# The shared expert's down products, moved from the combination into the first two passes of the expert loop

## The reference

```python
x = layer_norm(DEEPNORM_ALPHA * x + ffn, ln2_g[i], ln2_b[i])
# ffn, in moe_ffn, for each of 64 experts, with the tokens that chose it (6 experts a token):
hb = jax.nn.silu(xb @ w_gate[eb]) * (xb @ w_up[eb])
yb = hb @ w_down[eb]                      # weighed by the token's gate, and added up
shared = (jax.nn.silu(x2 @ w_sh_gate) * (x2 @ w_sh_up)) @ w_sh_down
return acc[:T] + shared
```

## Time and profile before

| | us |
|---|---|
| median of 3 runs | 2179.4 (2177.65 to 2179.82) |
| span of the profiled execution | 2182.5 |
| PE busy | 1923.4 (88%) |
| DVE busy | 802.0 (37%) |
| expert loop, first layer, first gate product to last down product | 431.0 to 975.0 |
| expert loop, second layer | 1571.8 to 2127.3 |

### The profile page before, as it was taken

The page is one execution under the profiler, slowest core; times in us unless marked ns, Lnnn a source line. Parts: engine busy times, 40 slices in busy tenths (PEclk is TensorE's granted clock), DMA queues, the critical chain, the costliest instruction groups (busy, mean ns, idle before and its releaser), DMA issues. The chain is left out here.

```text
span 2182.5 us, 32986 instructions
## 1 busy us (share of the span) xinstructions
PE 1923.4 (88%) x11132; PEld 1122.2 (51%) x11133; DVE 802.0 (37%) x2138; ACT 374.2 (17%) x840; POOL 292.3 (13%) x375
## 2 busy tenths in 40 slices
PE   9999999799888888788999779999799888877787
PEld 4575545356545554344444368865356454544443
DVE  3101643533222222226367644524533222222226
ACT  2001641011111110010344412211011011100011
POOL 6000000011111111110017231100011111111110
PEclk9999899899999999999999589998899999999999
DMA  6210110899999999965222110012769999999966
GB/s 232 77 59 9 69 63 39 307 351 421 418 421 390 421 392 421 421 269 226 68 71 65 25 26 1 21 58 108 303 257 419 421 421 391 421 421 422 420 286 274
DMA packets 143416, 540.50 MB, mean 248 GB/s; under 512 B 30814, under 2 KB 68246, under 8 KB 93550
## 3 DMA queue, kind: packets, MB, share of 16 engines
q1 hardware_dynamic: 122030, 489.14, 55.9%
q0 software_dynamic: 21312, 50.37, 6.1%
HBM read 521.06 MB, written 45.61 MB: 260 GB/s over the span
## 5 line engine op out<-in xcount | busy, mean ns | idle before, releaser
L632 PE MATMUL bank<-W,XT 128*64 128x256 f32 x4608 | 533.0, 387 | 102.2 <-DMA W<-in_w_exp_up_dram 46.9
L632 PEld LDWEIGHTS bank<-W,XT 128*64 128x64 f32 x4608 | 355.6, 139 | 301.1 <-DMA W<-in_w_exp_gate_dram 75.1
L667 PE MATMUL bank<-W,ht 128*64 128x512 f32 x1152 | 277.8, 626 | 43.5 <-DMA W<-in_w_exp_down_dram 38.6
L667 PEld LDWEIGHTS bank<-W,ht 128*64 128x64 f32 x1152 | 86.9, 143 | 177.0 <-issue 134.7
L1858 PE MATMUL bank<-XT,rin_w 128*128 128x512 f32 x352 | 156.5, 599 | 0.0
L1151 PE MATMUL bank<-XT,foxw 128*128 128x512 f32 x320 | 137.8, 592 | 0.0
L643 DVE TENSOR_TENSOR gu<-sig,bank 128x256 f32<-128x256 f32 x72 | 30.3, 421 | 287.3 <-ACT sig L639 287.2
L645 DVE TENSOR_TENSOR h<-gu,bank 128x256 f32<-128x256 f32 x72 | 30.3, 421 | 243.2 <-PE bank L632 243.1
L1858 PEld LDWEIGHTS bank<-XT,rin_w 128*128 128x128 f32 x352 | 66.4, 192 | 83.7 <-issue 83.3
L618 ACT ACTIVATE XT<-bank 128x512 f32<-128x512 f32 x74 | 44.2, 597 | 378.3 <-PE bank L610 378.3
L1151 PEld LDWEIGHTS bank<-XT,foxw 128*128 128x128 f32 x320 | 60.6, 190 | 76.4 <-issue 76.4
(11 more groups left out here) (409 smaller groups left out, 2497.6 us busy)
## 6 DMA issues: line engine op xcount, KB each, us to landing
W<-in_w_exp_gate_dram SPq DMA_DIRECT2D x128, 1024.0 KB, 18.7
W<-in_w_exp_up_dram SPq DMA_DIRECT2D x128, 1024.0 KB, 20.8
W<-in_w_exp_down_dram SPq DMA_DIRECT2D x128, 1024.0 KB, 18.9
W<-y_rows SPq DMA_DIRECT2D x8, 2048.0 KB, 15.4
foxw<-in_fox_w_in_dram SPq DMA_DIRECT2D x13, 1024.0 KB, 5.4
rin_w<-in_rwkv_w_in_dram SPq DMA_DIRECT2D x22, 512.0 KB, 4.1
W<-y_rows SPq DMA_DIRECT2D x8, 1024.0 KB, 22.2
w_out<-in_w_out_dram SPq DMA_DIRECT2D x1, 4096.0 KB, 13.0
```

The lines of the kernel that those rows point to most:

```text
L632: last = pe.matmul((gate, up)[m][64 * a:64 * a + 64, :], xt[s][:, k, 64 * a:64 * a + 64], K.W[:, w, a, m, k * FE:(k + 1) * FE], start=(k = ...
L667: last = pe.matmul(B[5 + half][64 * a:64 * a + 64, :], ht[:, j, 64 * a:64 * a + 64], K.W[:, w, a, 2, at:at + 512], start=(j == 0), stop=(j ...
```

## The change

- The 16 shared down products of a layer go from the combination into passes 0 and 1 of the expert loop, in 8 pieces of two matmuls, 4 pieces a pass. A piece is half a tile of tokens' output (128 x 512) in bank 4. In each pass the pieces stand behind `gate_up`, behind `turn_x`, behind `turn_h` and behind `down`. Both layers do this.
- Behind each piece DVE does `X = alpha * X + bank 4` on that half tile (one scalar_tensor_tensor of 128 x 512). PE starts a piece only when DVE has added the one before (`shared_added`).
- The four scalings of X by alpha go from the combination, and each routed sum starts its bank anew.
- The slots' numbers move from bank 4 to the free half of bank 7, which the up products use; PE therefore waits for `index_made` ahead of the up products.
- In pass 0, `slot_rows` and `index_rows` for pass 2 move behind the third piece.

```diff
@@ expert_loop
-        slots = B[4][:, 0:4]
+        slots = B[7][:, FE:FE + 4]
@@ gate_up
             for m, done in ((0, gate_done), (1, gate_up_done)):
+                if m:
+                    pe.wait_ge(index_made, n + 3 if not early(n) or n else 2)
@@ new
+        def shared_product(pe, piece):
+            t, half = divmod(piece, 2)
+            if piece == 0:
+                pe.wait_ge(shared.loaded, 16)
+            else:
+                pe.wait_ge(shared_added, piece)
+            for j in range(2):
+                last = pe.matmul(B[4][:], shared.hidden[:, j, t * P:(t + 1) * P], shared.w[:, j, half * 512:(half + 1) * 512],
+                                 start=(j == 0), stop=(j == 1))
+            last.then_inc(shared_made, 1)
+
+        def add_shared(dve, piece):
+            t, half = divmod(piece, 2)
+            dve.wait_ge(shared_made, piece + 1)
+            x = K.X[:, t, half * 512:(half + 1) * 512]
+            dve.scalar_tensor_tensor(x, x, ALPHA, B[4][:], ALU.mult, ALU.add).then_inc(shared_added, 1)
+
+        def early(n):
+            return isinstance(n, int)
@@ PE, from_slot
                         gate_up(pe, u, n, pair, w)
-                        if isinstance(n, int) and n == 0:
+                        if early(n):
+                            shared_product(pe, 4 * n)
+                        turn_x(pe, 1 - u, n + 1)
+                        if early(n):
+                            shared_product(pe, 4 * n + 1)
+                        turn_h(pe, n)
+                        if early(n):
+                            shared_product(pe, 4 * n + 2)
+                        if early(n) and n == 0:
                             slot_rows(pe, 0, 2)
-                        turn_x(pe, 1 - u, n + 1)
-                        turn_h(pe, n)
                         slot_rows(pe, 1 - u, n + 3)
                         down(pe, n, pair, w)
+                        if early(n):
+                            shared_product(pe, 4 * n + 3)
@@ DVE, one_pass (index_rows for pass 2 goes from ahead of the loop to here)
                     hidden(dve, n, step)
+                    if early(n):
+                        add_shared(dve, 4 * n)
                     keep_xt(dve, 1 - u, n + 1, 1)
+                    if early(n):
+                        add_shared(dve, 4 * n + 1)
                     keep_ht(dve, n)
-
+                    if early(n):
+                        add_shared(dve, 4 * n + 2)
+
+                    if early(n) and n == 0:
+                        index_rows(dve, 0, ahead[1][:, 2:3], 2, step)
...
                     keep_y(dve, u, n, 1)
+                    if early(n):
+                        add_shared(dve, 4 * n + 3)
@@ Combination.products
-        pe.wait_ge(self.scaled, 1)
-        pe.wait_ge(self.diagonals, 1)
-        pe.wait_ge(shared.loaded, 16)
...
-        for t in range(NT - 1):
-            shared_product(t)
-        pe.wait_ge(self.diagonals, NT * BY_TENSOR)
         for t in range(NT):
-            if t == 1:
-                shared_product(NT - 1)
+            pe.wait_ge(self.diagonals, (t + 1) * BY_TENSOR)
             pe.wait_ge(self.loaded_t[t], 16)
...
-                                     start=False, stop=(j == BY_TENSOR - 1))
+                                     start=(j == 0), stop=(j == BY_TENSOR - 1))
@@ Combination.sums
         for t in range(NT):
-            dve.tensor_scalar_mul(X[:, t, :], X[:, t, :], ALPHA).then_inc(self.scaled, 1)
-        for t in range(NT):
             dve.wait_ge(self.loaded_v[t], 16)
-            dve.wait_ge(self.scaled, t + 1)
```

More of the change, by code:

```diff
@@ L531, in expert_loop @@
         ht = sb("ht", [P, 2, P])
-        ending = Combination(K, L, scope, shared, out, next_weights)
-        slots = B[4][:, 0:4]
+        ending = Combination(K, L, scope, out, next_weights)
+        slots = B[7][:, FE:FE + 4]
         gate, up = B[2][:, 0:FE], B[7][:, 0:FE]
@@ L542, in expert_loop @@
         y_a, y_d = sem("y_a"), sem("y_d")
+        shared_made, shared_added = sem("shared_made"), sem("shared_added")
         stored = [sem("stored0"), sem("stored1")]
@@ L782, in _ @@
                 one_hot(dve, 1, 3)
-                index_rows(dve, 0, ahead[1][:, 2:3], 2, step)
-                start = step.n
+                start = step.n + 1
                 def one_pass(n, u):
-                    step = Chain(dve, steps, start + n * PASS_STEPS)
+                    step = Chain(dve, steps, start + n * PASS_STEPS - (1 if early(n) and n == 0 else 0))
                     hidden(dve, n, step)
+                    if early(n):
+                        add_shared(dve, 4 * n)
                     keep_xt(dve, 1 - u, n + 1, 1)
+                    if early(n):
+                        add_shared(dve, 4 * n + 1)
                     keep_ht(dve, n)
+                    if early(n):
+                        add_shared(dve, 4 * n + 2)
+                    if early(n) and n == 0:
+                        index_rows(dve, 0, ahead[1][:, 2:3], 2, step)
                     wait_from(dve, stored[u], through(n - 2, u))
@@ L805, with __init__ @@
 class Combination:
-    def __init__(self, K, L, scope, shared, out, next_weights):
+    def __init__(self, K, L, scope, out, next_weights):
         def sb(name, shape):
@@ L814, in sem @@
             return scope.sem(f"combine{L}_{name}")
-        self.K, self.shared, self.out, self.next_weights = K, shared, out, next_weights
+        self.K, self.out, self.next_weights = K, out, next_weights
         self.rows = K.arena.rearrange("p (t j d) -> p t j d", t=NT, j=TOPK)
@@ L820, in __init__ @@
         self.loaded_t = [sem(f"rows_t{t}") for t in range(NT)]
-        self.added, self.diagonals, self.summed, self.scaled, self.y_stored = (
-            sem(n) for n in ("added", "diagonals", "summed", "scaled", "y_stored"))
+        self.added, self.diagonals, self.summed, self.y_stored = (
+            sem(n) for n in ("added", "diagonals", "summed", "y_stored"))
         self.ln = LayerNorm(K, scope, f"ln2_{L}", K.in_["ln2_g"][L:L + 1, :], K.in_["ln2_b"][L:L + 1, :])
@@ L843, in products @@
     def products(self, pe):
-        B, shared = self.K.banks, self.shared
-        pe.wait_ge(self.scaled, 1)
-        pe.wait_ge(self.diagonals, 1)
-        pe.wait_ge(shared.loaded, 16)
[L849 to L853, removed]
-        for t in range(NT - 1):
-            shared_product(t)
-        pe.wait_ge(self.diagonals, NT * BY_TENSOR)
+        B = self.K.banks
         for t in range(NT):
-            if t == 1:
-                shared_product(NT - 1)
+            pe.wait_ge(self.diagonals, (t + 1) * BY_TENSOR)
             pe.wait_ge(self.loaded_t[t], 16)
```

## The result

The changed kernel is slower. Its median is 2213.4 us (5 runs, 2204.0 to 2214.8) against 2179.8 (5 runs); the ratio is 1.0144, with a 95% interval of 1.0129 to 1.0158, so +31.4 us (28 to 34). The forecast was +30.3. The profiled execution took 2208.4 us, 5 us under the median.

A forecast was written before the change was run, and what follows sets the result against it. Weights' transfers set the expert loops' length, but PE's first passes set when the dry DMA queue restarts. Loop starts +30.6 us and combinations -0.3 gave +30.3 on the median 2179.4: 2209.7 us, range 2201 to 2217.

The forecast's parts named there:

- Term 1: Start of each expert loop: pieces and waits in passes 0 and 1 delay pass 2 by 15.3 us a layer, 30.6 in all.
- Its split: Passes 0 and 1: 13.8 us a layer of products with no idle time to take them in; waits on top, 15.3 together.
- the walk: Second layer's pass 0, step by step from the last up product: down products 6.2 us later, pass 1 starts 7.9 late.
- The restart: Dry DMA queue early in each loop: its restart, and the loop's end, move by as much as PE's first passes lengthen.
- The rival that hides the start: Early passes of the loops: transfers and not PE decide, so the 15.3 us a layer disappear; 2175.3 us, chance 0.06.
- the one in which only one layer pays: Loop starts: the first layer's loop takes its 15.3 us in elsewhere; 2194.4 us, chance 0.05.
- The sign that I had named: Both expert loops: distance from first to last expert product longer by 15.3 us.
- Stalls: the rival: PE's stalls in pass 2 (first layer) and ahead of pass 3 (second) shrink, 5.4 us off; 2204.3 us, chance 0.12.
- The sum: Whole kernel: 30.6 us for the loop starts less 0.3 for the combinations, 30.3 us slower, 2209.7 us.
- Term 2: Combination: DVE gains 2.04 us a layer, the cold clock takes 1.9 back; 0.3 us gained in all.

The follow-up runs named there:

- start_pe: Kernel before, combination whole, with the 8 pieces also made in passes 0 and 1, without DVE additions or waits for them; ratio 1.0127, +27.7 us.
- late: Changed kernel with the same pieces and additions in passes 28 and 29 instead of 0 and 1; ratio 1.0022 to the kernel before, +4.8 us.
- spread: Kernel before with one more unused matmul behind the down products of each of the 34 looped passes of a layer; ratio 0.9996.
- again: Changed kernel run once more for a second profile, no edit; ratio 1.0152 to the kernel before, median 2211.0 us.
- after: Changed kernel in its first profile, against the kernel before; ratio 1.0144, median 2213.4 us.
- after_warm: Changed kernel with 24 records of unused products in PE's wait ahead of the combination's routed products; ratio 1.0120 to the kernel before.
- pad: Kernel before with 32 matmuls in pass 0's never-taken branch for slot 1; ratio 1.0039, +8.5 us.

## Why the prediction was right, point by point

**Term 1, 15.3 us a layer: right in its sum.** Measured 15.4 and 15.5 in both profiles of the changed kernel, and start_pe, late and spread show that it is paid for its place ahead of the restart. The steps hold too: the down products of pass 0 came 6.2 us late as forecast (9.44 behind the last up product for 3.27), pass 1 8.2 late where the sum had 7.9. The same pieces cost 31 to 33 us in passes 0 and 1 and 5 in passes 28 and 29.

**Its split was not right.** I wrote that PE had no idle time to take the pieces in, 13.8 us of products and 1.5 of waits. start_pe shows 11.8 for the products alone, so they do fill some 2 us of idle time, and the handshake with DVE and the later indices cost the other 3.6. The wait for the indices was 1.34 us; the walk has about 1.2 for it (1589.75 less 1587.97 and the 0.6 of the first slot rows). By the ratios, start_pe to the changed kernel is 5.4 us; by the traces 7.3.

**The restart: right.** The dry spells at 485 and 1645 to 1655 are there, and the loop behind the restart takes 492 to 494 us in both kernels. The rival that hides the start is out. So is the one in which only one layer pays: both starts lost the same. The sign that I had named, each loop 15.3 us longer from first to last expert product, did not come true as it stands: the loops grew by 11.9 and 20.2, in again by 11.6 and 16.7.

**Stalls: the rival was half right.** The 2.28 us in the first layer went, as that rival had it, with the clock that fell behind it. In the second layer they grew by 3.2 us, or 1.1 in the second profile. The sum had put the stalls at no change, with no row behind it, and they did change, in opposite directions: against the 30.9 us of the two starts, the loops of the profiles are 32.1 (after), 28.3 (again) and 24.8 (after_warm) longer. That the sum fits so well is luck in this part. The first layer's stall seems to go with the program and not with the execution: all ten profiles without pieces in passes 0 and 1 have one of 1.9 to 2.9 us in pass 2, and the four with pieces there have none, but up to 1.4 in pass 0. Why is not shown. The spread of the changed kernel's runs (11 us, against 5.8 before in the same comparison) may be the second layer's; that is argued and not shown. The Trainium skill (Runtime: NRT & Kernel Launch, section Instruction fetch mechanics) says that a taken branch to code outside the fetched pages waits for a fetch. pad is in line with it, with 7.71 us at the jump over 32 more matmuls instead of 1.80; that the jump's target lay outside the fetched pages no run here shows.

**Term 2, -0.3 us: right, and for the reason given.** The combinations of the changed kernel took 50.8 and 55.6 us against 50.6 and 55.8. DVE's wait of 2.04 us for tile 1 is gone, and its wait for tile 0 has grown. It was one of 1.38 us before, in both layers:

```profile
2146.69 0.69 DVE L887 TENSOR_TENSOR X<-X,bank 128x512 f32<-128x512 f32 x1 [1.38 <-PE bank L864]
```

In the second layer it is 0.90 and 2.67 now, 2.2 more (in the first 1.34 and 2.67, 2.6 more):

```profile
2163.62 30.11 PE L890 MATMUL bank<-W,diagonal 128*128 128x512 f32 x64 [12.07 <-DMA W<-y_rows]
...
2169.54 0.69 DVE L910 TENSOR_TENSOR X<-X,bank 128x512 f32<-128x512 f32 x1 [0.90 <-PE bank L890]
...
2172.90 0.69 DVE L910 TENSOR_TENSOR X<-X,bank 128x512 f32<-128x512 f32 x1 [2.67 <-PE bank L890]
...
2180.48 1.29 DVE L910 TENSOR_TENSOR X<-X,bank 128x512 f32<-128x512 f32 x2
```

The windows ahead of the first routed product and behind it (after the busy times the granted clock, DMA share, GB/s):

```profile
2160.00:2163.50 3.50, 0.00 (x0) 0.00 (x0) 0.00 (x0) 0.00 (x0) 0.00 (x0) 0.50 1.03 412
2163.50:2168.00 4.50, 4.38 (x6) 1.87 (x7) 1.93 (x2) 0.00 (x0) 0.00 (x0) 0.51 1.01 414
```

PE had nothing to do for 12.07 us, the granted clock was 0.50, 1.2 GHz, and tile 0's 16 records took 9.26 us, not 7.11, a loss of 2.15 where the forecast had 1.9. That time stands in the chain of waits (start, us, who):

```profile
2163.62 9.26 PE bank L890 x16
```

after_warm took it back. The Trainium skill (TensorE: Matmul & The Clock Gate, section HAM oscillation) says that waits for transfers between bursts of matmuls bring the clock down and that the next burst pays for it; the 12.07 us of idle time with 9.26 us behind it agree, and so do the 7.10 us of after_warm.

**The sum.** 30.3 forecast, 31.4 and 33 measured in two comparisons, both intervals with 30.3 inside. The stages without an edit shifted by more than this gap in single profiles, so I don't look for a cause of it.

## What to carry to other kernels

A stage that is bound by transfers has a start at which it is not yet bound by them: a queue that has run dry is waiting for the slowest thing in front of its restart, and work put there is paid nearly in full, while the same work behind the restart can be free (29 us a layer of it were). So don't ask what bounds the loop but what released the first transfer after the last dry spell. And work that seems to be hidden in a wait may be keeping the clock up for what follows: leave something in its place.

## What the runs showed of the hardware that I had not expected

Instructions that never run can cost time: 32 matmuls in a branch not taken made the jump over them stall for 7.71 and 4.77 us instead of 1.8, and the kernel 8.5 us slower. Smaller stalls without a releaser (1 to 4 us) stood at other places in each kernel; whether they are of that kind is not shown. They did not repeat in size between two executions of the changed kernel, so that differences of 5 us between kernels of this size need their stages compared and not their totals.
